# A two-block transformer on one core: the attentions of the second block rearranged

## The reference, cut to what matters

```python
h = _rms(x, norm1)
z = h @ w_in                                   # 1024 -> 2572 columns
(aq, ak, av, bq, bk, bv, bf, cq, ck, cv, ci, cf, co) = _split_in_proj(z)
aq = _rope(_rms(aq.reshape(B, S, 8, 64), swa_q_norm), pos)      # ak likewise, 2 heads
ya = _swa_attention(aq, ak, av, sinks)         # windowed softmax with a sink per head
bq = _rms(bq.reshape(B, S, 4, 64), fox_q_norm) # bk likewise
log_f = log_sigmoid(bf + fox_f_bias)
yb = _fox_attention(bq, bk, bv, log_f)         # scores + F_i - F_j, causal softmax
hc = _mlstm(cq, ck, cv, ci + i_bias, cf + f_bias)
#   Dm = causal(b_i - b_j + ig_j); m = max(inter, max_j Dm); Sm = (q k^T) * exp(Dm - m)
#   h = (Sm v) / max(|sum_j Sm|, exp(-m))      # with a state carried from chunk to chunk
yc = sigmoid(co) * _rms(hc, mlstm_out_norm)
x = x + concat([ya, yb, yc]) @ w_out
u = _rms(x, norm2) @ w_ff1
x = x + square(relu(u)) @ w_ff2
```

## Time and profile before

| what | value |
|---|---|
| median of 3 runs | 1862.65 us (1858.8, 1862.65, 9115.66) |
| the profiled execution | 1862.39 us, its span 1861.1 us |
| PE | 1678.8 us busy, 90% of the span |
| DVE | 852.3 us, 46% |
| ACT | 685.3 us, 37% |
| instructions | 23119 |
| transfers | 393.85 MB, mean 212 GB/s |
| mean granted TensorE clock | 0.939 |

### The profile page before, as it was taken

The page is one execution under the profiler, slowest core; times in us unless marked ns, Lnnn a source line. Parts: engine busy times, 40 slices in busy tenths (PEclk is TensorE's granted clock), DMA queues, the critical chain, the costliest instruction groups (busy, mean ns, idle before and its releaser), DMA issues. The chain is left out here.

```text
span 1861.1 us, 23119 instructions
## 1 busy us (share of the span) xinstructions
PE 1678.8 (90%) x9672; PEld 1285.2 (69%) x9672; DVE 852.3 (46%) x1545; ACT 685.3 (37%) x1075; POOL 29.1 (2%) x49
## 2 busy tenths in 40 slices
PE   7998999998889999999998988578999886789999
PEld 6788996433337888995443357457999785469998
DVE  6575564010035575554011056553555464545554
ACT  4445541111123455431111144633444446235443
POOL 4000000000000000000000000000000000000000
PEclk9999999999999999999999999758999997579999
DMA  9443458799984442568799964102555342024553
GB/s 302 146 150 114 159 214 322 305 422 421 418 354 150 141 142 106 206 253 334 304 421 422 418 243 163 65 1 99 193 183 185 130 162 91 1 86 152 192 182 113
DMA packets 58276, 393.85 MB, mean 212 GB/s; under 512 B 7220, under 2 KB 7264, under 8 KB 16048
## 3 DMA queue, kind: packets, MB, share of 16 engines
q1 hardware_dynamic: 55008, 381.35, 54.0%
q0 software_dynamic: 3008, 9.61, 1.9%
q10 hardware_dynamic: 144, 1.30, 0.2%
HBM read 391.18 MB, written 1.05 MB: 211 GB/s over the span
## 5 line engine op out<-in xcount | busy, mean ns | idle before, releaser
L1593 DVE TENSOR_TENSOR ring_rounded<-ring_sb,ring_rounded 128x2048 fp32r<-128x2048 f32 (+4 forms) x180 | 385.7, 2156 | 232.8 <-ACT ring_rounded L1215 232.5
L1215 ACT ACTIVATE ring_rounded<-ring_sb 128x2048 fp32r<-128x2048 f32 (+4 forms) x180 | 322.1, 1803 | 199.6 <-PE psum L590 166.6
L590 PE MATMUL psum<-ring_sb,region_sb 128*64 128x512 f32 x1440 | 333.0, 602 | 29.3 <-DMA ring_sb<-in_weights 20.4
L590 PE MATMUL psum<-xT_hi_rounded,ring_rounded 128*128 128x256 f32 x1920 | 349.5, 284 | 0.0
L590 PEld LDWEIGHTS psum<-xT_hi_rounded,ring_rounded 128*128 128x128 f32 x1920 | 300.2, 192 | 0.6
L590 PE MATMUL psum<-ring_rounded,region_rounded 128*128 128x512 f32 x1184 | 290.2, 396 | 6.0 <-DVE memory_kv_rounded L2244 3.0
L590 PE MATMUL psum<-xT_lo_rounded,ring_rounded 128*128 128x256 f32 x960 | 274.8, 286 | 5.8 <-DVE xT_lo_rounded L2030 5.8
L590 PEld LDWEIGHTS psum<-ring_sb,region_sb 128*64 128x64 f32 x1440 | 107.4, 138 | 231.2 <-issue 228.9
L590 PEld LDWEIGHTS psum<-ring_rounded,region_rounded 128*128 128x128 f32 x1184 | 224.6, 191 | 55.3 <-issue 3.8
L590 PE MATMUL psum<-ring_rounded,xT_hi_rounded 128*128 128x384 f32 (+4 forms) x832 | 232.2, 356 | 17.9 <-DVE ring_rounded L1593 11.4
L590 PEld LDWEIGHTS psum<-xT_lo_rounded,ring_rounded 128*128 128x128 f32 x960 | 184.6, 192 | 8.7 <-DVE xT_lo_rounded L2030 6.2
(11 more groups left out here) (265 smaller groups left out, 1454.1 us busy)
## 6 DMA issues: line engine op xcount, KB each, us to landing
ring_sb<-in_weights SPq DMA_DIRECT2D x312, 1024.0 KB, 7.7
ring_sb<-in_weights SPq DMA_DIRECT2D x24, 768.0 KB, 4.4
ring_sb<-in_weights SPq DMA_DIRECT2D x8, 904.0 KB, 4.6
ring_sb<-in_weights SPq DMA_DIRECT2D x8, 900.0 KB, 4.6
region_sb<-in_weights SPq DMA_DIRECT2D x6, 1024.0 KB, 10.5
ring_sb<-in_weights SPq DMA_DIRECT2D x8, 584.0 KB, 9.5
region_sb<-in_mem_turned POOLq DMA_DIRECT2D x2, 1024.0 KB, 7.3
region_sb<-in_pool_band POOLq DMA_DIRECT2D x2, 1024.0 KB, 9.6
```

Source lines behind the costliest of these rows:

```text
L590: return nc.tensor.matmul(dst, lhsT, rhs, start=first, stop=last, skip_group_check=True)
L1215: nc.scalar.activation(rounded(piece.hi), piece.raw, ACT.Copy).then_inc(hi_made, 1)
L1593: nc.vector.tensor_tensor(rounded(piece.raw), piece.raw, reread(piece.hi), ALU.subtract).then_inc(lo_made, 1)
```

## The change

It leaves what is computed as it is and rearranges the second block's attention half:

- The input columns are stored in another order (swa queries, keys, values, the 12 gates, fox queries and keys, mlstm queries and keys, output gates and fox values, mlstm values) and cut at 512, 268, 512, 512, 512 and 256 columns.
- VectorE norms, rotates and squares both token blocks in one instruction. The fox gains are multiplied into the scale of ScalarE's copy of the turned queries.
- The scores of several heads share a bank: four heads of 128 keys or two of 256, even and odd heads in different banks.
- The maximum of a row comes out of the masking instruction; the fox and mlstm rows no longer add the decay of the query's own position, which cancels, and the floor of mlstm is formed from it apart.
- Probabilities are turned undivided. All values are made by rows (128 columns of probabilities held), divided on the way out of PSUM, and turned (`pe_turn_y`); upper and lower parts follow for 512 columns at a time.
- Where the diff leaves lines out of the lists, the decay sums (after cut 2), the key rows (after the first scores) and the squares of the fox heads (after the rotation) stand. TensorE turns swa heads between the halves of cut 3, the others' heads and the first probabilities between those of cut 4, the second ones between those of cut 5; the decay sums stand behind cut 2. The output product is made over the first 512 inputs (swa) for one column half, then the other, before the mlstm values are normed, and over the rest at the end; the plan of pieces follows it.
- Sigmoid of the output gate becomes Tanh of half, with `(tanh + 1) * gain` and a factor 0.5 in the last multiplication.
- Feed-forward: ScalarE makes the upper part by Square of the Relu output; VectorE squares into another buffer.
- First block: the bias is loaded twice, ScalarE and VectorE make an upper and a lower row of it, and one fp32r product of two rows adds it.

```diff
-C2_AQ, C2_AK, C2_AV, C2_BQ, C2_BK, C2_BV, C2_BF = 0, 512, 640, 768, 1024, 1280, 1536
+C2_AQ, C2_AK, C2_AV, C2_GATES, C2_BQ, C2_BK, C2_CQ, C2_CK, C2_CO, C2_BV, C2_CV = 0, 512, 640, 768, 780, 1036, 1292, 1548, 1804, 2060, 2316
-Z2_CUTS = even_cuts(C2_AQ, C2_BQ, 2) + even_cuts(C2_BQ, IN2, 4)
+Z2_CUTS = [(C2_AQ, C2_AK), (C2_AK, C2_BQ), (C2_BQ, C2_CQ), (C2_CQ, C2_CO), (C2_CO, C2_CV), (C2_CV, IN2)]
...
             for half in range(2):
+                if half and between:
+                    between()
...
-                            last = matmul(psum[:, i, 0:n], upto[0:1, 0, P:S], bias, False, True)
+                            last = matmul(psum[:, i, 0:n], rounded(ones), rounded(bias), False, True)
...
+        def pe_value_rows(key, b, heads, probsT, values, ready, read):
+            i, free, full = loose.take(key, read)
+            pe.wait_ge(*ready)
+            pe.wait_ge(*free)
+            for h in range(heads):
+                for kb in range(b + 1):
+                    last = matmul(psum[:, i, h * HD:(h + 1) * HD], probsT[:, h, kb * P:(kb + 1) * P], values(h, kb), kb == 0, kb == b)
+            last.then_inc(full, 1)
@@ tensor_second @@
+            cut(2)
...
+            cut(3, turn_swa)
+            pe_swa_scores(l, 0)
...
+            pe_swa_scores(l, 1)
+            cut(4, turn_others)
+            pe_mls_gates(l, 0)
+            pe_fox_scores(l, 0)
+            pe_mls_gates(l, 1)
+            pe_swa_values(l, 0)
+            cut(5, lambda: swa_probs(1))
+            pe_fox_scores(l, 1)
+            pe_swa_values(l, 1)
+            pe_mls_scores(l, 0)
+            pe_mls_scores(l, 1)
+            fox_probs(0)
+            pe_turn_y(l, 0, 0)
+            fox_probs(1)
+            pe_turn_y(l, 0, 1)
+            mls_probs(0)
+            pe_fox_values(l, 0)
+            mls_probs(1)
+            pe_attended(l, 0, 0)
+            pe_fox_values(l, 1)
+            pe_mls_values(l, 0)
+            pe_mls_values(l, 1)
+            pe_attended(l, 0, 1)
+            pe_turn_y(l, 1, 0)
+            pe_turn_y(l, 1, 1)
+            pe_attended(l, 1, 0)
+            pe_attended(l, 1, 1)
@@ vector_second @@
+            head_squares("swa", z2[:, :, C2_AQ:C2_AV], swa["scratch"], SWA_HEADS + SWA_KV, swa_summed)
+            decay_gates()
+            round_lo(first + 8)
+            swa_heads()
+            decay_logs()
+            round_lo(first + 9)
+            swa_rope()
...
+            round_lo(first + 10)
+            fox_heads()
+            decay_keys()
+            round_lo(first + 11)
+            swa_scores(0)
+            decay_rows()
+            swa_scores(1)
+            round_lo(first + 13)
+            mls_gates(0)
+            fox_scores(0)
+            mls_gates(1)
+            swa_values(0)
+            mls_gain()
+            round_lo(first + 15)
@@ scalar_second @@
+            act_exps(swa["probs"][1], SWA_HEADS, S, softmax_stats("swa", 1, SWA_HEADS), swa_lowered.at(l, 1), 1.0, swa_exped)
+            act_sink(l, 1)
+            cut(4)
...
-                    nc.scalar.activation(rounded(hiddenT[j % 2][0][:, f, :]), upT[f % 2][:, :], ACT.Copy).then_inc(hidden_hi.sem, 1)
+                    nc.scalar.activation(rounded(hiddenT[j % 2][0][:, f, :]), upT[f % 2][:, :], ACT.Square).then_inc(hidden_hi.sem, 1)
...
+            round_lo(first + 2)
+            v.wait_ge(consts_in, 16)
+            nc.vector.tensor_copy(rounded(ones), upto[0:2, 0, P:S]).then_inc(ones_made.sem, 1)
+            v.wait_ge(*bias_upper_made.at(l))
+            nc.vector.scalar_tensor_tensor(rounded(bias_rows), reread(bias_upper), ident[0:2, 1:2], bias_rows, ALU.mult,
+                                           ALU.add).then_inc(bias_made.sem, 1)
             round_lo(first + 3)
```

More of the change, by code:

```diff
@@ L297, in weight_plan @@
             plan += [(w, True) for w in halves("w_in_2", (l,), (0, D), cut, "rows")]
-        for a in (0, BANK):
-            plan += [(w, True) for w in halves("w_out_2", (l,), (0, D), (a, a + BANK), "rows")]
+        both = [halves("w_out_2", (l,), (0, D), (a, a + BANK), "rows") for a in (0, BANK)]
+        plan += [(both[half][part_], True) for part_ in range(2) for half in range(2)]
         for j in range(0, D_FF + BANK, BANK):
@@ L1070, in pe_fox_scores @@
         def pe_fox_scores(l, b):
             keys = (b + 1) * P
-            for h in range(FOX_HEADS):
-                i, free, full = loose.take(("fox", l, b, h), fox_scored.at(l, b * 4 + h))
-                at = HD * (h % 2)
-                pe.wait_ge(*fox_qk_made.last(l))
+            groups = bank_heads(b, FOX_HEADS)
+            banks = [loose.take(("fox", l, b, n), fox_scored.at(l, b * 4 + max(group))) for n, group in enumerate(groups)]
+            pe.wait_ge(*fox_qk_made.last(l))
+            pe.wait_ge(*key_rows_made.at(l))
@@ new lines, in pe_fox_scores @@
+            for _, free, _ in banks:
+                pe.wait_ge(*free)
+            for place in range(2):
+                for (i, _, full), group in zip(banks, groups):
+                    h = group[place]
+                    at = HD * (h % 2)
+                    dst = psum[:, i, place * keys:(place + 1) * keys]
+                    matmul(dst, fox["qT"][at:at + HD, h // 2, b * P:(b + 1) * P], fox["kT"][at:at + HD, h // 2, 0:keys], True, False)
+                    last = matmul(dst, row_of(h, 8), key_rows[:, 0:keys], False, True)
+                    if place:
+                        last.then_inc(full, 1)
@@ L1090, in pe_mls_scores @@
+                last.then_inc(full, 1)
         def pe_mls_scores(l, b):
             keys = (b + 1) * P
-            for h in range(MLSTM_HEADS):
-                i, free, full = loose.take(("mls", l, b, h), mls_scored.at(l, b * 4 + h))
-                at = HD * (h % 2)
-                pe.wait_ge(*mls_qk_made.last(l))
+            groups = bank_heads(b, MLSTM_HEADS)
+            banks = [loose.take(("mls", l, b, n), mls_scored.at(l, b * 4 + max(group))) for n, group in enumerate(groups)]
+            pe.wait_ge(*mls_qk_made.last(l))
@@ L1546, in scalar_second @@
             act_sink(l, 1)
[L1547 to L1548 removed]
+            cut(4)
+            a.wait_ge(*z2_made.at(l, 9))
+            nc.scalar.activation(mls["opened"], z2[:, :, C2_CO:C2_CO + 256], ACT.Tanh, scale=0.5).then_inc(mls_open.sem, 1)
             act_mls_weights(l, 0)
[L1550 to L1552 removed]
@@ L2105, in decays @@
[L2105 to L2117 removed]
+                nc.vector.reciprocal(sums, sums).then_inc(*vs.next())
```

607 lines of the change are left out of this document (323 added, 284 removed).

## The result

The changed kernel takes **1759.85 us** (median of 4 runs, 1758.37 to 1762.2), the kernel before beside it 1864.42 (median of 4 runs): a ratio of **0.9448 [0.9436, 0.9460]**, about 103 us less. One run of the kernel before, of 9115.66 us, is left out of the ratio. The forecast was 1768 (1732 to 1814), faster. Its profiled execution spans 1758.6 us against 1861.1.

The account below looks back on a forecast made before the run. The second block's attentions were taken as bound by a to-and-fro chain between engines at a low TensorE clock. Attentions 76, bias 14 and feed-forward 4 sum to 94 us off 1862, so 1768 us (1732 to 1814).

Parts of the forecast that it names:

- I lean slightly to the low end: Second block's attentions: choice of 38 us gained per layer, 76 in all, between 23 at low and 57 at upper clock.
- A: Second-block attention stage, from the first projection product to the start of cut 4: laid at 54 us, upper clock.
- B: Second-block attention stage, from cut 4 to the end of cut 5, with transposes, gates and scores: laid at 30 us.
- C: Second-block attention stage, from the end of cut 5 to the first output product, all small work: laid at 16.5 us.
- D: Second-block attention stage, output product in parts with the mlstm values between: laid at 28.5 us.
- upper clock throughout: Rival for the second block's attentions: upper clock holds, 57 us gained a layer, 1727 us (to 1740); chance 0.12.
- low clock: Rival for the second block's attentions: clock stays low, 23 us gained a layer, 1802 us (1790 to 1820); chance 0.24.
- new wait behind a weight piece's halves: Around cuts 4 and 5: VectorE's gates wait behind a piece whose upper half ScalarE makes after eight exponentials; 2.1 us.
- 17 in all, since TensorE is filled there: First block's bias products: 8.4 us saved a layer, 17 in all; net 14 after making the rows (10 to 17).
- The feed-forward: ScalarE's Square without waiting for VectorE shortens a 3.0 us TensorE wait per layer: 2 a layer, 4 us (0 to 6).
- The edits eat each other: Rival: swa and fox chains queue with the rounding, projection waits and gives back most of the tail; 1826 to 1862; 0.10.
- slower: Rival: in the projection, new VectorE and ScalarE blocks come between weight pieces and products; 1868, or 1900; chance 0.04.

Follow-up runs that it names:

- experiments 6: Changed kernel with cuts 4 and 5 made at once after cut 3 and the small work behind them: 1780.14 us, 0.9556 to the kernel before.
- 7: Changed kernel with the transposes of cuts 3, 4 and 5 behind their cut instead of between its halves: 1776.33 us, 0.9531 to the kernel before.
- 8: Changed kernel with one head to a bank in all scores and gates, instead of two or four: 1776.75 us, 0.9537 to the kernel before.
- experiment 3: Kernel before without the first block's bias products, 14 unused products added in layer 0's router: 1856.48 us, 0.9963 to the kernel before.
- Experiment 5: Changed kernel with the feed-forward's square undone (VectorE squares, ScalarE copies again): 1763.81 us, 0.9476 to the kernel before.

## Why the prediction came out as it did

**The attentions: right in mechanism, too small by 28.** The term was 2 times 38 = 76, between 23 and 57 a layer; measured are 54.0 and 49.6, near the upper bound. The step that was off is "I lean slightly to the low end", with the earlier trace rows's 0.56 taken as the nearest row for the small work. By stages: A was laid at 54 and took 48.6, at a clock of 1.00 throughout, with the 2.9 us for a low start not lost. B was laid at 30 and took 34.3 at 0.85, C at 16.5 and took 21.1 at 0.68, D at 28.5 and took 29.0. So the rival "upper clock throughout" holds in A and D, the rival "low clock" in parts of B and C. With 1.2 and 2.4 GHz as the two levels, 0.85 over 34.3 us and 0.68 over 21.1 us are 10 and 14 us at the lower one, where before it was some 97 us a layer (twice 70.9 by 0.09, 92.2 by 0.44 and 23.9 by 0.07). The price of the low clock belonged on B and C alone. The rows that said so were there: 0.91 and 0.93 beside 0.56 in the earlier trace rows, dense cuts near the upper level beside the small work. Gaps are not needed for the lower level: in B and C TensorE is busy all of the time. Value products of B and of C, with no idle time ahead of them:

```profile
1506.54 3.67 PE L603 MATMUL psum<-region_sb 128*128 128x64 f32 x16
1524.52 10.11 PE L603 MATMUL psum<-region_sb 128*128 128x64 f32 x48
```

3.67 us for 16 is what the earlier trace rows has at the lower level.

The 2.1 us that B had for a new wait behind a weight piece's halves came as nothing here. But the chain it named is the one that experiments 6, 7 and 8 brought up, with 3.5 to 5.3 us a layer.

**The transposes did not pull the clock down.** The forecast weighed this against the 0.58 us products behind the 12 transposes and the 6.0 us gap in the earlier trace rows. The changed kernel parts the two; TensorE's timeline between the halves of cut 4, its first two rows the 24 transposes (one row between the last two left out):

```profile
1490.26 1.91 PE L655 MATMUL psum<-consts_sb,region_sb 128*128 128x128 f32 x16
1492.00 1.04 PE L758 MATMUL psum<-consts_sb,region_sb 128*128 128x128 f32 x8
1492.80 0.48 PE L603 MATMUL psum<-ring_rounded,xT_hi_rounded 128*128 128x512 f32 x1
1493.34 0.62 PE L603 MATMUL psum<-ring_rounded,xT_hi_rounded 128*128 128x512 f32 x2
```

The products behind them start at their upper-level pitch, and the window from 1489.80 is granted 1.00. And 12 transposes behind a wait of only 0.9 us, in cut 3, are at the upper level themselves:

```profile
1472.60 1.53 PE L655 MATMUL psum<-consts_sb,region_sb 128*128 128x128 f32 x12 [0.87 <-DVE region_sb L2202]
```

In the earlier trace rows the 12 take 2.82, so the clock was down before they began. The drop there thus goes with the gap of 6.0 us ahead of them. The Trainium skill, *TensorE: Matmul & The Clock Gate*, Part 4, says that transposes do not count as activity for the clock. This trace can't say whether they count; 2.5 us of them among products, with no gap, cost no clock.

**ScalarE's tables: 0, as costed.** The stage has five loads of 1.28 us where nine were counted before, TensorE waits for none of them, and there is none at the line of the Tanh (L1667), between exponentials. That agrees with the Trainium skill, *ScalarE: Activation LUTs*, Table sets, which puts exp and tanh into one set.

**The bias: wrong, and by nearly all of its size.** Failing step: "17 in all, since TensorE is filled there (slices of nine tenths)". Two things were wrong in it. The products' saving was sized by ratio at 8.4 a layer; the groups of layer 0's bias products in the changed kernel (busy, mean ns, idle before)

```profile
L603 PE MATMUL psum<-region_rounded 2*128 2x384 f32 x8 | 3.5, 434 | 0.0
L603 PE MATMUL psum<-region_rounded 2*128 2x292 f32 x4 | 1.6, 396 | 0.4 <-DVE region_rounded L1955 0.4
L603 PE MATMUL psum<-region_rounded 2*128 2x512 f32 x2 | 1.0, 500 | 0.0
```

are 6.1 us where they were 12.5 before, so 6.4. And a slice of nine tenths is not a full one: with all 12.5 us away, experiment 3 got 7 us for two layers. VectorE was next in line, and the granted clock fell, in the mixings and in the experts behind them. Of the rest, the making of the two rows takes 2.6 us at the start (TensorE's wait on the weights' rounding 14.0 instead of 11.4), as costed. In the changed kernel layer 0's mixing is 2.5 us shorter, layer 1's no shorter, and layer 0's experts are 5 longer, by the second stop and a lower clock.

**The feed-forward: 4, within its range of 0 to 6.** Experiment 5 loses 4 us by the medians and 3.9 by the spans, 3.2 of them in layer 0 (from the end of the output product to layer 1's first projection product 198.1 us instead of 194.9). Against the kernel before, the two feed-forwards are only 1.5 us shorter; what in the rest of the change takes back the difference was not looked into. One reading was wrong: TensorE does not wait once per layer for this chain. The 3.0 us stand in layer 0's feed-forward alone, where 2.1 are left, and layer 1's has no such wait.

**The rivals.** "The edits eat each other" and "slower" wanted TensorE to wait on weight halves between the cuts; no such wait is in the stage's list, and with 1.5 us more on VectorE only 1.4 us of waiting came. How near it was, experiments 6 to 8 show: there a weight half does hold up VectorE's gates, and through them TensorE. Of the sum, the attentions were 28 us too small, the bias 16 too large and the feed-forward by the traces 2.5: the three together leave 9, so 1768 against 1760 looks better than its terms were.

## What to carry to other kernels

Between engines that hand work to and fro, put the hand-over under half of a dense product block: the place of 12 to 24 transposes was worth 8 us a layer, with not one operation removed. Then look at what else stands in the other engines' lists there: the longest wait of three experiments was on a weight piece's rounding that happened to stand ahead of the gates. Price a low clock by stretches (dense products, small products, with gaps or without), not by one mean. And before counting a saving on a "nine tenths" engine as time, find the next wait behind it: leaving the work out altogether tells about what a faster form of it can give, and the clock has to be read with it.

## What the runs showed of the hardware that was not expected

TensorE can stop for 2.5 to 4.0 us with nothing to wait for in the profile, at the start of a group of products in layer 0's experts, while weights fill the DMA engines; seven unused products far ahead of that place took the second stop away. Code that is merely moved can so cost or give 2.5 us by the spans, 6 by the ratios (0.9982 against 1.0015 for the same edit), of 1860.

One fp32 bias product of 512 columns, a pair of passes, holds TensorE for 1.05 us; with two rows in one pass it is recorded at 0.50.

The granted clock can take back what TensorE saves. With 12.5 us less of products a layer in the first block, five of five runs have a lower mean clock than any of the nine beside them (0.933 to 0.936 against 0.937 to 0.941), which is up to 9 us of the upper level in 1856.
